# Gated split combine in an expert layer: four-pass products replaced by single-pass pairs, VectorE's row sums and permutations spread over three blocks

## What is computed

```
logits = einsum('bsd,de->bse', h, w_router);  top_val, top_idx = top_k(logits, 2)
gates  = sum(one_hot(top_idx) * softmax(top_val))
for e in range(8):
    out = out + gates[..., e:e+1] * (silu(h @ w1[e]) * (h @ w3[e])) @ w2[e]
```

## Time and profile before

| | us |
|---|---|
| median of 3 runs (1688.45 to 1691.34) | 1689.2 |
| the profiled execution, its own time | 1688.66 |
| its span in the profile | 1686.8 |
| TensorE busy in the span | 1643.1 (97%) |
| VectorE busy | 1279.4 (76%) |
| ScalarE busy | 1054.2 (62%) |
| mean DMA rate | 268 GB/s |

### The profile page before, as it was taken

How to read it: one execution, slowest core, us unless ns; L and a number is a source line. 1 busy time by engine, 2 the same in 40 slices (tenths; PEclk the granted TensorE clock), 3 DMA queues, 4 the chain that set the end, 5 groups by cost and what they waited for, 6 DMA issues and landing times.

```text
span 1686.8 us, 25150 instructions
## 1 busy us (share of the span) xinstructions
PE 1643.1 (97%) x9630; PEld 1425.2 (84%) x9630; DVE 1279.4 (76%) x1072; ACT 1054.2 (62%) x902; POOL 62.1 (4%) x60
## 2 busy tenths in 40 slices
PE   7999989999899998999999999999999999999998
PEld 6998989999898997788788788788788788788787
DVE  5974754555795466987987987987887887887886
ACT  5444454545544536677677677677677677677675
POOL 0121100000023010000000000000000000000000
PEclk9999999999999998999999999999999999999999
DMA  9543455566353342899999899899899899999893
GB/s 331 165 148 102 126 175 183 191 199 198 125 169 109 125 151 83 323 383 333 330 378 338 328 374 342 326 379 338 326 378 339 325 379 338 328 377 338 321 383 145
DMA packets 231292, 452.46 MB, mean 268 GB/s; under 512 B 6992, under 2 KB 80720, under 8 KB 231120
## 3 DMA queue, kind: packets, MB, share of 16 engines
q1 hardware_dynamic: 231248, 451.82, 75.5%
HBM read 450.74 MB, written 1.05 MB: 268 GB/s over the span
## 4 chain that ended last, share of the span: by engine, by line
PE 88%; DVE 7%; ACT 2%; issue 2%; DMA 1%; DVEq 0%; SPq 0%; ACTq 0%
PE bank L275 27%; PE bank L277 26%; PE bank L276 26%; DVE w_low L265 3%; PE bank L1260 2%; ACT w_high L261 1%; PE bank L1276 1%; DVE xacc L941 1%; DMA raw<-w_in 1%; PE bank L1097 1%; PE bank L1009 1%; PE bank L1099 0%; PE bank L1116 0%; PE bank L1060 0%; PE bank L1098 0%
## 5 line engine op out<-in xcount | busy, mean ns | idle before, releaser
L265 DVE TENSOR_TENSOR w_low<-raw,w_high 128x2048 fp32r<-128x2048 f32 x427 | 975.6, 2291 | 281.7 <-ACT w_high L261 280.9
L261 ACT ACTIVATE w_high<-raw 128x2048 fp32r<-128x2048 f32 x427 | 818.9, 1918 | 399.7 <-PE bank L277 396.6
L275 PE MATMUL bank<-w_high,hg_high 128*128 128x512 f32 x896 | 354.5, 396 | 8.5 <-DVE w_low L265 8.5
L277 PE MATMUL bank<-w_high,hg_low 128*128 128x512 f32 x896 | 349.6, 390 | 0.0
L276 PE MATMUL bank<-w_low,hg_high 128*128 128x512 f32 x896 | 349.2, 390 | 0.0
L275 PE MATMUL bank<-h_high,w_high 128*128 128x256 f32 x1056 | 299.9, 284 | 6.2 <-DVE h_low L618 4.8
L277 PE MATMUL bank<-h_high,w_low 128*128 128x256 f32 x1056 | 293.5, 278 | 0.0
L276 PE MATMUL bank<-h_low,w_high 128*128 128x256 f32 x1056 | 293.5, 278 | 0.0
L275 PEld LDWEIGHTS bank<-h_high,w_high 128*128 128x128 f32 x1056 | 199.3, 189 | 11.7 <-issue 9.4
L275 PEld LDWEIGHTS bank<-w_high,hg_high 128*128 128x128 f32 x896 | 168.5, 188 | 44.6 <-DVE w_low L265 10.7
L276 PEld LDWEIGHTS bank<-h_low,w_high 128*128 128x128 f32 x1056 | 199.1, 189 | 1.6 <-issue 1.4
(11 more groups left out here) (236 smaller groups left out, 1584.0 us busy)
## 6 DMA issues: line engine op xcount, KB each, us to landing
raw<-exp_w SPq DMA_DIRECT2D x336, 1024.0 KB, 6.0
raw<-w_in SPq DMA_DIRECT2D x42, 1024.0 KB, 5.1
raw<-ffn_w SPq DMA_DIRECT2D x33, 1024.0 KB, 5.3
raw<-w_out SPq DMA_DIRECT2D x8, 1024.0 KB, 5.2
raw<-w_br_attn SPq DMA_DIRECT2D x4, 1024.0 KB, 5.0
raw<-w_br_pool SPq DMA_DIRECT2D x2, 1024.0 KB, 4.9
raw<-w_br_conv SPq DMA_DIRECT2D x2, 1024.0 KB, 5.1
cst<-consts SPq DMA_DIRECT2D x1, 1280.0 KB, 14.7
```

What stands on the lines that cost most here:

```text
L261: nc.scalar.activation(wh[c % SPLIT][:], raw[c % RAW][:], ACT.Copy).then_inc(s["high_done"], 1)
L265: nc.vector.tensor_tensor(wl[c % SPLIT][:], raw[c % RAW][:], wh[c % SPLIT][:].bitcast(F32), ALU.subtract).then_inc(s["split_done"], 1)
L275: pe.matmul(dst, lh, rh, start=start and i == 0, stop=False)
L277: last = pe.matmul(dst, ll, rh, start=False, stop=stop and i == len(terms) - 1)
```

## The change

1. The combine is made of single-pass products. ScalarE copies banks 2 and 3 to `ysH` (F32R), multiplied by the gate of the slot (`gslot`, a column of 128), and VectorE writes `ysL` = bank * gate - ysH (new `y_low`, two instructions of 128x512). `permT` is now F32R and holds a plain permutation, so each of the four results is two F32R matmuls, permT x ysH and permT x ysL.
2. `gslot` is computed at a job's end by two float32 matmuls of one column (`permC` x `gcol`), behind the two transposes, and copied by ScalarE. `gcol` is a VectorE copy of 128x2.
3. The zero products go: the first `down` of a job starts the accumulation. For this TensorE's first middle block is written out ahead of the loop.
4. VectorE's four adds and four permutation instructions are no longer in a row at the job's start: one add stays there, two go into the first block, the last add and `perm` into the second, `permC` and `gcol` into the third. VectorE's first three blocks are written out. Split c+4 goes ahead of `mult`.
5. `turn` waits for the first add alone; the gathers wait for all four.
6. Job 0 skips `y_out` and `y_low`: two memsets of 128x1024 provide zeros in `ysH` and `ysL` instead, ahead of the routing. The memset of `zero` there goes (128x512).

```diff
                 def y_out(j):
-                    act.wait_ge(s["m_zero"], 1)
                     act.wait_ge(s["used"], j * JOB_PIECES + MOE0)
+                    act.wait_ge(s["m_ptout"], j * 2 + 2)
                     for h in range(2):
-                        nc.scalar.activation(ysb[:, 512 * h:512 * h + 512], bank[2 + h][:], ACT.Copy).then_inc(s["m_yout"], 1)
+                        nc.scalar.activation(ysH[:, 512 * h:512 * h + 512], bank[2 + h][:], ACT.Copy,
+                                             scale=gslot[:]).then_inc(s["m_yhigh"], 1)
...
                     nc.scalar.activation(permT[:], bank[1][:, 0:S], ACT.Copy).then_inc(s["m_ptout"], 1)
+                    nc.scalar.activation(gslot[:], bank[1][:, S:S + 1], ACT.Copy).then_inc(s["m_ptout"], 1)
...
-                nc.vector.memset(zero[:].bitcast(F32), 0.0).then_inc(s["zeros"], 1)
-                nc.vector.memset(permT[:], 0.0).then_inc(s["m_ptout"], 1)
+                nc.vector.memset(permT[:].bitcast(F32), 0.0).then_inc(s["m_ptout"], 2)
+                nc.vector.memset(ysH[:].bitcast(F32), 0.0).then_inc(s["m_yhigh"], 2)
+                nc.vector.memset(ysL[:].bitcast(F32), 0.0).then_inc(s["m_ylow"], 2)
...
+                def y_low(j):
+                    for h in range(2):
+                        dve.wait_ge(s["m_yhigh"], j * 2 + (h + 1))
+                        nc.vector.scalar_tensor_tensor(
+                            out=ysL[:, 512 * h:512 * h + 512], in0=bank[2 + h][:], scalar=gslot[:],
+                            in1=ysH[:, 512 * h:512 * h + 512].bitcast(F32), op0=ALU.mult,
+                            op1=ALU.subtract).then_inc(s["m_ylow"], 1)
+
                 def job(j):
                     r0, c = j * EXP_BLOCKS, MOE0
                     for k in range(SPLIT if isinstance(j, int) else 0, 4):
                         split_low(dve, c + k, r0)
+                    if not isinstance(j, int):
+                        y_low(j)
+                    split_low(dve, c + 4, r0)
                     mult(r0 + 1, j * JOB_PIECES + (MOE0 + 4))
-                    split_low(dve, c + 4, r0)
                     split_low(dve, c + 5, r0)
-                    add_rows(j * 4)
-                    make_perm(0, perm, j + 1)
-                    make_perm(2, permG, j)
-                    with dve.Fori(0, EXP_BLOCKS - 1) as i:
+                    add_rows(j * 4, 0)
+
+                    def middle(i, at=None):
                         r = j * EXP_BLOCKS + i
                         split_low(dve, c + 6, r)
                         split_low(dve, c + 7, r)
+                        if at == 0:
+                            add_rows(j * 4, 1)
+                        elif at == 1:
+                            add_rows(j * 4, 3)
                         split_low(dve, c + 8, r)
                         t_low(r + 1)
                         split_low(dve, c + 9, r)
                         mult(r + 2, r * RAW + (MOE0 + 8))
                         split_low(dve, c + 10, r)
+                        if at == 0:
+                            add_rows(j * 4, 2)
+                        elif at == 1:
+                            make_perm(0, perm, j + 1)
+                        elif at == 2:
+                            make_perm(0, permC, j)
+                            nc.vector.tensor_copy(gcol[:].unsqueeze(2), jobs[:, 2, :, bass.ds(j, 1)]).then_inc(s["m_gate"], 1)
                         split_low(dve, c + 11, r)
+
+                    for i in range(3):
+                        middle(i, i)
+                    with dve.Fori(3, EXP_BLOCKS - 1) as i:
+                        middle(i)
...
                 def combine(count):
                     for q, b in enumerate((4, 7, 5, 6)):
-                        ins = pe.matmul(bank[b][:], permT[:, (q // 2) * P:(q // 2) * P + P],
-                                        ysb[:, 512 * (q % 2):512 * (q % 2) + 512], start=True, stop=True)
+                        for y in (ysH, ysL):
+                            ins = pe.matmul(bank[b][:], permT[:, (q // 2) * P:(q // 2) * P + P],
+                                            y[:, 512 * (q % 2):512 * (q % 2) + 512], start=y is ysH, stop=y is ysL)
                         ins.then_inc(s["m_comb"], 1)
...
                     combine(j * 4)
-                    zero_bank(2)
-                    zero_bank(3)
...
-                        pe.wait_ge(s["m_add"], j * 4 + 4)
+                        if first:
+                            pe.wait_ge(s["m_add"], j * 4 + 1)
                         turn(r + 1)
...
                     pe.wait_ge(s["m_silu"], r0 + EXP_BLOCKS)
+                    pe.wait_ge(s["m_add"], j * 4 + 4)
                     for g in range(4):
                         gather(g)
...
                     for t in range(TT):
-                        ins = pe.transpose(bank[1][:, t * P:t * P + P], permG[:, t, :], ident)
+                        ins = pe.transpose(bank[1][:, t * P:t * P + P], permC[:, t, :], ident)
+                    pe.wait_ge(s["m_gate"], j + 1)
+                    for t in range(TT):
+                        ins = pe.matmul(bank[1][:, S:S + 1], permC[:, t, :], gcol[:, t:t + 1], start=t == 0, stop=t == TT - 1)
                     ins.then_inc(s["m_permt"], 1)
```

More of the change, by code:

```diff
@@ L187, in trunk @@
         xacc = sb("xacc", [P, TT, D])
-        ysb = sb("ysb", [P, D])
-        permG = sb("perm_gated", [P, TT, P])
-        permT = sb("perm_t", [P, S])
+        ysH = sb("ys_high", [P, D], F32R)
+        ysL = sb("ys_low", [P, D], F32R)
+        permC = sb("perm_copy", [P, TT, P])
+        permT = sb("perm_t", [P, S], F32R)
         perm = sb("perm", [P, TT, P], F32R)
@@ L203, in trunk @@
         jobi = sb("jobi", [P, 16], I32)
+        gcol = sb("gate_column", [P, TT])
+        gslot = sb("gate_of_slot", [P, 1])
         names = """const_in high_done split_done used
@@ L558, in job @@
                             split_high(act, c + k, r0)
-                    y_out(j)
+                        y_out(j)
                     split_high(act, c + 3, r0)
@@ L988, in experts @@
                     job(j)
-                add_rows(njobs * 4)
+                y_low(njobs)
+                for q in range(4):
+                    add_rows(njobs * 4, q)
             nc.vector.memset(warm[:], 1.0).then_inc(s["ones_set"], 1)
@@ L1277, in turn, with down @@
                     ins.then_inc(s["m_t"], 1)
-                def down(c, r, count, stop=False):
+                def down(c, r, count, start=False, stop=False):
                     pe.wait_ge(s["m_low"], count)
@@ L1286, in down @@
                                  H[:, k, 512 * n:512 * n + 512], L[:, k, 512 * n:512 * n + 512]) for k in range(2)],
-                                start=False, stop=stop and half_ == 1)
+                                start=start and half_ == 0, stop=stop and half_ == 1)
                         ins.then_inc(s["used"], 1)
@@ L1300, in experts @@
                     gather(g)
-                pe.wait_ge(s["zeros"], 2)
                 pe.wait_ge(s["fill_act"], 12)
-                for n in range(2):
-                    ins = pe.matmul(bank[2 + n][:], zero[:, 0:P], zero[:], start=True, stop=True)
-                ins.then_inc(s["m_zero"], 1)
                 def job(j):
@@ L1311, in job, with middle @@
                     up(c + 2, r0, 1)
-                    pe.wait_ge(s["m_yout"], j * 2 + 2)
-                    pe.wait_ge(s["m_ptout"], j + 1)
+                    pe.wait_ge(s["m_yhigh"], j * 2 + 2)
+                    pe.wait_ge(s["m_ylow"], j * 2 + 2)
+                    pe.wait_ge(s["m_ptout"], j * 2 + 2)
                     combine(j * 4)
-                    zero_bank(2)
-                    zero_bank(3)
-                    with pe.Fori(0, EXP_BLOCKS - 1) as i:
+                    def middle(i, first=False):
                         r = j * EXP_BLOCKS + i
@@ L1320, in job @@
                         up(c + 4, r, 0)
-                        pe.wait_ge(s["m_add"], j * 4 + 4)
+                        if first:
+                            pe.wait_ge(s["m_add"], j * 4 + 1)
                         turn(r + 1)
                         up(c + 6, r, 1)
-                        down(c + 8, r, r + 1)
+                        down(c + 8, r, r + 1, start=first)
+                    middle(0, first=True)
+                    with pe.Fori(1, EXP_BLOCKS - 1) as i:
+                        middle(i)
                     turn(j * EXP_BLOCKS + EXP_BLOCKS)
@@ L1340, in experts @@
                     job(j)
-                pe.wait_ge(s["m_yout"], njobs * 2 + 2)
-                pe.wait_ge(s["m_ptout"], njobs + 1)
+                pe.wait_ge(s["m_yhigh"], njobs * 2 + 2)
+                pe.wait_ge(s["m_ylow"], njobs * 2 + 2)
+                pe.wait_ge(s["m_ptout"], njobs * 2 + 2)
                 combine(njobs * 4)
```

11 lines of the change are left out of this document (5 added, 6 removed).

## The result

| | before | after |
|---|---|---|
| median of the runs, us | 1689.0 (1688.45 to 1691.34, 4 runs) | **1670.4** (1667.06 to 1673.42, 4 runs) |
| ratio, 95% interval | 1 | 0.9878 (0.9857 to 0.9898) |
| the profiled execution, its own time | 1688.66 | 1673.39 |
| one job, start to start | 126.69 | 123.61 |

1668.0 was forecast, with 1663 to 1675 as the range. The four times after stand in two groups, 1667.1 and 1667.3, 1673.4 and 1673.4; the profiled execution is one of the upper.

What follows compares the result with a forecast made beforehand. TensorE was taken as the bound, carrying 88% of the chain of waits. Terms -16.6 - 8.5 + 3.6 + 0.7 - 0.4 = -21.2 took 1688.66 to 1667.5; the median, 0.5 higher, was forecast at 1668.0 us, range 1663 to 1675.

Steps and rivals of the forecast that it cites:

- The combine: TensorE at each job's start: eight F32R products replace float32 matmuls and zero products, 2.08 us a job, -16.6 in all.
- the rival in which they don't: Combine's F32R products run at the float32 pace, 13 us lost, 1681 us; chance 2%.
- The gate products: Two one-column float32 matmuls on TensorE's path at each job's end, 0.45 us a job, +3.6 in all.
- the gate rival: Gate's way over ScalarE exceeds the 0.6 us margin: 0.5 to 1 us a job, 1672 to 1676; chance 5%.
- The wait for c+6: TensorE's 1.07 us idleness before piece c+6 in each job's first block goes by VectorE's new order, -8.5 in all.
- What is spread: VectorE's adds and permutation instructions put between splits fit the 0.89 us margin at `ge_low`: cost 0.
- Ahead of job 0: Before the first job, two larger memsets replace one on VectorE and delay the chain to `perm`: +0.7 us.
- Tail: Behind the last job, from ScalarE's copies to the fourth add: that add comes earlier, -0.4 us.
- the wait stays: VectorE's chain is slower than walked, so the 1.07 us before c+6 remain: 1676.5 us; chance 7%.

Runs made afterwards that it cites:

- experiment 7: Changed kernel with the pair of one-column gate products made three times over: 1674.9 us, 0.9921 of before.
- experiment 2: Kernel before with VectorE's new order and `turn` waiting for the first add, float32 combine and zero products kept: 1679.0 us, 0.9942 of before.
- experiment 8: Changed kernel with the three remaining adds in a row behind split c+7 of the first block: 1672.9 us, 0.9893 of before.
- experiment 5: Changed kernel with the three memsets moved ahead of the last norm on VectorE: 1665.9 us, 0.9853 of before.
- experiment 3: Changed kernel with split c+4 behind the product (`mult`) again: 1679.9 us, 0.9943 of before.
- experiment 4: Changed kernel run once more without any edit: 1666.6 us, 0.9860 of before.
- experiment 11: Changed kernel run again without any edit, for comparison on the same chip: 1668.5 us, 0.9869 of before.
- experiment 1: Changed kernel with VectorE's old order (product ahead of split c+4, adds and permutations in a row): 1699.6 us, 1.0056 of before.
- experiment 10: Experiment 9 plus four products of zeros in TensorE's pause for the first permutation: 1662.4 us, 0.9843 of before.
- experiment 9: Changed kernel with earlier memsets, two zero products ahead of first `up`, eight filling products and last combine by column halves: 1667.0 us, 0.9858 of before.

## Why the prediction was right, point by point

**The combine, -2.08 a job:** measured 2.08. F32R products with `permT` as weights have the pace of the others; the rival in which they don't is out.

**The gate products, +0.45 a job:** measured 0.45, and 0.45 again in experiment 7. What queues behind them on ScalarE shows in no wait: after's list has none for `w_high` or `w_low`, so the gate rival is out too.

**The wait for c+6, -1.07 a job:** the walk of VectorE's order was right to a few tenths (margin at c+6 1.7, as said; the two `y_low` from 927.96 to 929.27, so 0.65 each, as taken), and no new wait came. The size was off: the term was the idle record. From the transposes to c+6 it is 1.32, by experiment 2 a job gains 1.36. Over eight jobs this is 2.3 us more than the 8.5 of the sum.

**What is spread, 0:** right. 0.6 fits into the margin of 0.89; three adds in one place would not (experiment 8).

**Ahead of job 0, +0.7:** the failed step, +2.5 came. The memsets' part was about right (0.74 more of pause, gathers 0.85 later; 0.6 comes back in experiment 5). Missing was the price of removing the two zero products ahead of the first `up`, of which the prediction says nothing. They stood where TensorE has to wait for ScalarE's copy of `hg_low`. Without them TensorE pauses 0.73 us, and the 1.2 GHz level holds 3.4 us longer, 1.7 us of products. The prediction took nothing for the clock and kept 3 us on both sides, which held it. Up to 0.6 of the 2.5 can be the spread seen in experiment 2.

**Tail, -0.4:** the other failed step, +0.5 to +1.3 by the copy of `permT`, +0.1 to +0.9 by the last `down` (0.37 of the former is the copy's own move). Three things were missed. The two gated copies take 1.26 us and not 1.09, and the second `y_low` ends 2.1 us behind the start of the first copy where 1.8 was walked. Behind the fourth add 0.3 more pass where the adds run in a row. And the step priced the last combine at the full clock, which three of the profiles of the same tail have throughout (experiments 3, 5 and 8) and the profiled execution doesn't. TensorE's pause ahead of it grew from 1.25 to 2.35 us in all of them:

```profile
1664.79 0.47 PE L1326 MATMUL bank<-ys_high,perm_t 128*128 128x512 f32 x1 [2.35 <-ACT ys_high L543]
...
1666.94 0.63 PE L1326 MATMUL bank<-ys_high,perm_t 128*128 128x512 f32 x1
1667.37 0.63 PE L1326 MATMUL bank<-ys_low,perm_t 128*128 128x512 f32 x1
```
```profile
1666.00:1668.00 2.00, 2.00 (x5) 0.99 (x3) 1.59 (x3) 0.00 (x0) 0.00 (x0) 0.50 0.39 145
```

The clock fell to 0.50, the last products run 0.43 apart, a pair every 0.86. That is the pace the float32 products had at the full clock in the earlier trace rows: in this execution the new combine at the very end has no faster products than the old. In experiment 4 six of the eight run at the full pace, and the fourth add starts 4.8 us behind the first copy, against 4.95 before and 4.5 as walked: of the 0.5 walked 0.2 came there, and none of it at the end of the program.

**The errors offset:** the jobs gained 3.3 us more than the sum had (2.3 of it the wait), start and tail cost 3.1 more. The sum was -21.2 for -21.4. That it came so close is luck: two errors of 3 us, with different causes, cancel. That the median came 2.4 above the forecast goes with the pace of the dense layer (seen in the trace of one of the two upper runs), which no step had; 1666.6 of experiment 4 and 1668.5 of experiment 11 stand on both sides of 1668.0.

**The rivals:** "the wait stays" names the right danger. It takes one swapped line to bring a wait back, at c+4 (experiment 3), and with the old order the kernel is slower than before (experiment 1). That case was not among the rivals, since the change brings both halves; it is what this change would have been without its order.

## What to carry to other kernels

Where a shorter piece on the bounding engine is followed by work for which another engine is the supplier, move the supplier's order in the same change: here the faster products alone cost 0.6%, the order alone gave 0.6%, both together 1.2 to 1.4%. Read what a stall costs from start to start of the neighbours (1.67 to 0.35), not from its idle record (1.07). And before removing work of the bounding engine beside a pause, look at the granted clock there: two products of zeros, "useless" by the reference, cost nothing where they stood, and the 0.73 us of pause that replaced them cost 1.7 us by the clock.

## What was not expected of the hardware

- Products of zeros can keep the clock up. With four of them in the pause for `perm` and two behind the gathers the granted clock stays 1.00 (one profile, experiment 10) through a stretch in which the 1.2 GHz level held 6.8 us before and 10.2 us in the changed kernel. With the two alone it is 6.8.
- The 256-column products of the dense layer have two paces, 0.113 and 0.118 us, at the same granted clock of 1.00, drawn per execution, traced for the changed kernel and experiment 9: 6 us of the whole. It was only located, not explained.
- A copy from a bank with the gate as its scale takes 0.68 us on ScalarE (before without it 0.59), and VectorE's `y_low` 0.74 against 0.68 for `ge_low` of the same size: with a factor from a column, 128x512 costs 0.09 us more on ScalarE and 0.06 on VectorE, where the operation is also another one.
